# A transformer layer's first microseconds: the first norm's weights as one small row spread by TensorE, blocks in pairs, and transposes of the identity in between

## What is computed

```python
def _rmsnorm(x, g):
    y = x32 * lax.rsqrt(jnp.mean(x32 * x32, axis=-1, keepdims=True) + EPS)
    return (y * g.astype(jnp.float32)).astype(x.dtype)
...
    h = _rmsnorm(x, norm1_g)
    proj = jnp.einsum('bsd,de->bse', h, w_in)
    q, k, v, xr, gate = jnp.split(proj, [...], axis=-1)
```

## Time and profile before

| | |
|---|---|
| median of 3 runs | 1037.27 us |
| the profiled execution, its own time | 1037.77 us |
| its span, first to last instruction | 1035.8 us |
| TensorE busy in the span | 984.3 us (95%) |
| VectorE busy | 816.8 us (79%) |
| ScalarE busy | 745.8 us (72%) |

### The profile page before, as it was taken

One profiled execution on the slowest core, in us unless ns is written; L12 is line 12 of the kernel. 1 busy time (PEld: TensorE's weight loads), 2 busy tenths in 40 slices (PEclk: granted clock), 3 DMA queues, 4 the chain that ended last, 5 costly groups with the idle time before them and its releaser, 6 DMA issues.

```text
span 1035.8 us, 15188 instructions
## 1 busy us (share of the span) xinstructions
PE 984.3 (95%) x5051; PEld 825.9 (80%) x5051; DVE 816.8 (79%) x1084; ACT 745.8 (72%) x1004; POOL 336.8 (33%) x176
## 2 busy tenths in 40 slices
PE   5999999999999999949999999999999999999995
PEld 4997998877877888738888888888888888888874
DVE  5759898989885225777988988898889888988883
ACT  6448888488995555547877887797779777977773
POOL 1100000043792111140425642563366336503321
PEclk9999999999999999969999999999999999999998
DMA  8110111001102733379999999999999999999842
GB/s 285 38 47 6 46 42 42 0 2 62 62 1 84 274 113 118 129 268 412 409 392 391 410 392 392 391 411 392 391 389 401 388 390 387 399 385 364 307 168 35
DMA packets 75409, 248.97 MB, mean 240 GB/s; under 512 B 9396, under 2 KB 16616, under 8 KB 75368
## 3 DMA queue, kind: packets, MB, share of 16 engines
q1 hardware_dynamic: 70616, 231.65, 58.0%
q0 software_dynamic: 4752, 16.78, 6.5%
HBM read 231.63 MB, written 16.78 MB: 240 GB/s over the span
## 4 chain that ended last, share of the span: by engine, by line
PE 83%; DVE 7%; ACT 4%; issue 3%; POOL 1%; DMA 1%; ACTq 0%; SPq 0%; POOLq 0%; DVEq 0%
PE bank L1005 25%; PE bank L1007 24%; PE bank L1006 24%; PE bank L1011 5%; DVE e_lo L1687 2%; ACT e_hi L930 2%; PE bank L1187 1%; PE bank L1153 1%; PE bank L1154 1%; DMA x_nat<-in_x_prompt_dram 1%; PE bank L1040 1%; POOL prob L635 1%; POOL wo_lo L627 0%; DMA xs<-h_rows,idx_all 0%; DVE xc L1456 0%
## 5 line engine op out<-in xcount | busy, mean ns | idle before, releaser
L1005 PE MATMUL bank<-e_hi,xsT_hi 128*128 128x512 f32 x512 | 200.9, 392 | 1.2 <-DVE xsT_lo L1692 1.0
L1007 PE MATMUL bank<-e_hi,xsT_lo 128*128 128x512 f32 x512 | 199.3, 389 | 0.0
L1006 PE MATMUL bank<-e_lo,xsT_hi 128*128 128x512 f32 x512 | 199.3, 389 | 0.0
L667 POOL COPY idx_now<-idx_all 128x1 uint32 (+1 forms) x15 | 156.9, 10460 | 21.9 <-DMA y_dram<-ys,idx_now 21.9
L930 ACT ACTIVATE e_hi<-raw_gate 128x1024 fp32r<-128x1024 f32 x128 | 134.6, 1061 | 33.2 <-PE bank L1007 31.7
L1687 DVE TENSOR_TENSOR e_lo<-raw_down,e_hi 128x1024 fp32r<-128x1024 f32 x128 | 146.9, 1218 | 2.3
L1687 DVE TENSOR_TENSOR e_lo<-raw_up,e_hi 128x1024 fp32r<-128x1024 f32 x128 | 146.7, 1214 | 1.5 <-ACT e_hi L930 1.5
L1687 DVE TENSOR_TENSOR e_lo<-raw_gate,e_hi 128x1024 fp32r<-128x1024 f32 x126 | 145.7, 1216 | 2.5 <-ACT e_hi L930 2.5
L930 ACT ACTIVATE e_hi<-raw_up 128x1024 fp32r<-128x1024 f32 x128 | 126.5, 1058 | 1.7 <-PE bank L1007 0.3
L930 ACT ACTIVATE e_hi<-raw_down 128x1024 fp32r<-128x1024 f32 x128 | 125.1, 1058 | 1.3 <-PE bank L1007 1.2
L1005 PEld LDWEIGHTS bank<-e_hi,xsT_hi 128*128 128x128 f32 x512 | 96.1, 188 | 21.6 <-DVE xsT_lo L1692 1.2
(11 more groups left out here) (247 smaller groups left out, 2235.8 us busy)
## 6 DMA issues: line engine op xcount, KB each, us to landing
raw_gate<-in_exp_w_gate_dram SPq DMA_DIRECT2D x64, 1024.0 KB, 12.4
raw_up<-in_exp_w_up_dram SPq DMA_DIRECT2D x64, 1024.0 KB, 9.0
raw_down<-in_exp_w_down_dram SPq DMA_DIRECT2D x64, 1024.0 KB, 8.3
w_raw<-in_w_in_dram SPq DMA_DIRECT2D x6, 1024.0 KB, 5.4
wo_raw<-in_w_out_dram SPq DMA_DIRECT2D x8, 512.0 KB, 4.1
y_dram<-x SPq DMA_DIRECT2D x8, 512.0 KB, 5.1
h_rows<-h SPq DMA_DIRECT2D x8, 512.0 KB, 2.7
x_nat<-in_x_prompt_dram SPq DMA_DIRECT2D x4, 512.0 KB, 7.8
```

What stands on the lines that cost most here:

```text
L667: pool.tensor_copy(idx_now[:, 2:3], idx_all[:, bass.ds(e, 1)] if not isinstance(e, int) else idx_all[:, e:e + 1]).then_inc(idx_copied, 1)
L1005: pe.matmul(out, l_hi, r_hi, start=first, stop=False)
L1006: pe.matmul(out, l_hi, r_lo, start=False, stop=False)
L1007: return pe.matmul(out, l_lo, r_hi, start=False, stop=last)
```

## The change

The load of `g1b` by SyncE is gone. ScalarE, as its first instruction, issues a load of the same 1024 weights as 8 rows of 128 (`g1_rows`). TensorE transposes them to a [128, 8] tile, VectorE copies that to SBUF (`g1_cols`), and TensorE transposes each column, read as a 128 by 128 tile with the column repeated, so that banks 2 and 3 hold the weights on every partition. The norm of blocks 0 to 3 reads them from PSUM; ScalarE then copies them to `g1b` (step `gain`), and blocks 4 to 7 read that. SyncE loads all eight blocks ahead of the second weights and the vector rows. The list of steps takes the blocks in pairs. GpSimd makes the identity before its other constants. `keep_busy(n)` is new: n transposes of the identity into bank 0, whose result nobody reads; there are 6, 14, 4 and 14 of them.

```diff
@@ -128,6 +128,8 @@
     g1b = at("g1b", SM, [P, D], F32)
+    g1_rows = at("g1_rows", SM + 12 * K, [D // P, P], F32)
+    g1_cols = at("g1_cols", SM + 12 * K + 512, [P, D // P], F32)
@@ -299,22 +301,21 @@
-    steps = [("square_x", 0), ("norm_x", 0), ("square_x", 1), ("norm_x", 1), ("turn_x", 0), ("turn_x", 1),
-             ("w_hi", 0, 0), ("w_lo", 0, 0), ("hi_x", 0), ("lo_x", 0), ("w_hi", 0, 1), ("w_lo", 0, 1)]
-    for b in range(2, NB + 1):
-        if b < NB:
-            steps += [("square_x", b), ("norm_x", b)]
-        steps += [("hi_x", b - 1), ("lo_x", b - 1)]
-        if b < NB:
-            steps.append(("turn_x", b))
-        if b == 3:
-            steps.append(("vectors",))
-        if b == 6:
-            steps += [("w_hi", 1), ("w_lo", 1)]
-        steps.append(("project_pair", b - 2))
-        if b == 6:
-            steps += [("empty", 0), ("empty", 1)]
-    steps += [("project_pair", NB - 1), ("empty", 2), ("conv", 0)]
+    GAIN_FROM = 4
+    AHEAD = (6, 14, 4, 14)
+    steps = [("square_x", 0), ("norm_x", 0), ("turn_x", 0), ("square_x", 1), ("norm_x", 1), ("keep_busy", AHEAD[2]), ("turn_x", 1),
+             ("keep_busy", AHEAD[3]), ("w_hi", 0, 0), ("w_lo", 0, 0), ("hi_x", 0), ("lo_x", 0), ("hi_x", 1), ("lo_x", 1),
+             ("w_hi", 0, 1), ("w_lo", 0, 1), ("project_pair", 0), ("square_x", 2), ("norm_x", 2), ("square_x", 3), ("norm_x", 3)]
+    for b in range(2, NB, 2):
+        steps += [("turn_x", b), ("turn_x", b + 1)]
+        if b + 2 < NB:
+            steps.append(("square_x", b + 2))
+        steps += [("hi_x", b), ("lo_x", b), ("hi_x", b + 1), ("lo_x", b + 1)]
+        if b == 2:
+            steps.append(("gain",))
+        if b + 2 < NB:
+            steps += [("norm_x", b + 2), ("square_x", b + 3),  ("norm_x", b + 3), *([("vectors",)] if b == 4 else []), ("project_pair", b - 1), ("project_pair", b)]
+    steps += [("w_hi", 1), ("w_lo", 1), ("project_pair", 5), ("empty", 0), ("empty", 1), ("project_pair", 6), ("project_pair", 7), ("empty", 2), ("conv", 0)]
@@ -499,19 +500,16 @@
         load_x(0)
-        sp.dma_start(g1b[:, :], norm1_g[0:1, :].to_broadcast([P, D])).then_inc(g1_loaded, 16)
         load_x(1)
...
-        for b in range(2, BPS):
+        for b in range(2, NB):
             load_x(b)
         sp.dma_start(w1_raw[:, :, :], w_in[0, :, GROUPS[1][2]:GROUPS[1][2] + GW].rearrange("(k p) n -> p k n", p=P)).then_inc(w1_loaded, 16)
         for at_row, rows_in in rows:
             sp.dma_start(vec_rows[at_row:at_row + rows_in.shape[0], :], rows_in).then_inc(vec_loaded, 16)
-        for b in range(BPS, NB):
-            load_x(b)
@@ -600,12 +598,12 @@
         pool.memset(eps, EPS).then_inc(pool_ready, 1)
+        pool.wait_ge(ident_zeroed, 1)
+        pool.affine_select(out=ident[:, :], in_=ident[:, :], compare_op=ALU.not_equal, fill=1.0, base=0,
+                           pattern=[[-1, P]], channel_multiplier=1).then_inc(pool_ready, 1)
...
-        pool.wait_ge(ident_zeroed, 1)
-        pool.affine_select(out=ident[:, :], in_=ident[:, :], compare_op=ALU.not_equal, fill=1.0, base=0,
-                           pattern=[[-1, P]], channel_multiplier=1).then_inc(pool_ready, 1)
@@ -732,6 +730,7 @@
+        act.dma_start(g1_rows[:, :], norm1_g[0].rearrange("(c p) -> c p", p=P)).then_inc(g1_loaded, 16)
@@ -742,6 +741,10 @@
+            elif kind == "gain":
+                act.wait_ge(xn_ready, GAIN_FROM)
+                act.wait_ge(vec_t, 2)
+                act.activation(g1b[:, :], bank[:, 2:4, :].rearrange("p a b -> p (a b)"), ACT.Copy).then_inc(vec_copied, 1)
@@ -1027,9 +1030,24 @@
-        pe.wait_ge(pool_ready, 5)
+        def keep_busy(n):
+
+            for _ in range(n):
+                pe.transpose(bank[:, 0, 0:P], ident[:, :], ident[:, :])
+
+        pe.wait_ge(pool_ready, 2)
+        keep_busy(AHEAD[0])
+        pe.wait_ge(g1_loaded, 16)
+        pe.transpose(bank[:, 1, 0:D // P], g1_rows[:, :], ident[0:D // P, 0:D // P]).then_inc(vec_t, 1)
+        pe.wait_ge(vec_copied, 1)
+        for c in range(D // P):
+            ins = pe.transpose(bank[:, 2 + c // 4, c % 4 * P:(c % 4 + 1) * P], g1_cols[:, c:c + 1].to_broadcast([P, P]), ident[:, :])
+        ins.then_inc(vec_t, 1)
+        keep_busy(AHEAD[1])
@@ -1043,6 +1061,8 @@
                 pe.wait_ge(ht_lo_done, BPS * (t + 1))
+                if arg[0] in (4, 5):
+                    pe.wait_ge(vec_copied, arg[0] - 2)
@@ -1053,8 +1073,8 @@
                 pe.wait_ge(vec_loaded, 6 * 16)
+                pe.wait_ge(vec_copied, 2)
                 pe.transpose(bank[:, 3, 0:VECS], vec_rows[:, :], ident[0:VECS, 0:VECS]).then_inc(vec_t, 1)
-                pe.wait_ge(vec_copied, 1)
@@ -1382,7 +1402,9 @@
-        dve.wait_ge(g1_loaded, 16)
+        dve.wait_ge(vec_t, 1)
+        dve.tensor_copy(g1_cols[:, :], bank[:, 1, 0:D // P]).then_inc(vec_copied, 1)
+        dve.wait_ge(vec_t, 2)
@@ -1392,8 +1414,11 @@
+                if b >= GAIN_FROM:
+                    dve.wait_ge(vec_copied, 2)
+                gain = bank[:, 2:4, :].rearrange("p a b -> p (a b)") if b < GAIN_FROM else g1b[:, :]
                 dve.scalar_tensor_tensor(out=x_norm[:, b % 2, :], in0=x_nat[:, b, :], scalar=rstd1[:, b:b + 1],
-                                         in1=g1b[:, :], op0=ALU.mult, op1=ALU.mult).then_inc(xn_ready, 1)
+                                         in1=gain, op0=ALU.mult, op1=ALU.mult).then_inc(xn_ready, 1)
```

More of the change, by code:

```diff
@@ L1028, in turn_heads @@
             transposes(turn_bank(n), pieces, qkT_done)
-        pe.wait_ge(pool_ready, 5)
+        def keep_busy(n):
[10 more added lines that the diff above has]
+        keep_busy(AHEAD[1])
         for step in steps:
             kind, arg = step[0], step[1:]
+            if kind == "keep_busy":
+                keep_busy(*arg)
             if kind == "turn_x":
@@ L1415, in _ @@
             elif kind == "vectors":
-                dve.wait_ge(vec_t, 1)
+                dve.wait_ge(pool_ready, 5)
+                dve.wait_ge(vec_t, 3)
                 dve.tensor_copy(vecs[:, :], bank[:, 3, 0:VECS]).then_inc(vec_copied, 1)
-                dve.wait_ge(vec_copied, 1)
+                dve.wait_ge(vec_copied, 3)
             elif kind == "softplus":
```

## The result

The changed kernel takes 1031.82 us, the median of 4 runs (1031.07 to 1032.55), beside 1037.38 for the kernel before (4 runs, 1036.99 to 1038.49). The ratio is 0.9945, with an interval of 0.9934 to 0.9957: 5.6 us faster, 0.55%. The prediction said 1032.0.

A forecast was written before the change was run, and what follows sets the result against it. VectorE was taken to hold back TensorE's first product. Stage's end: 12.8 + 28.34 + 0.1 + 0.2 + 0.5 = 41.9 against 47.23, 5.3 us less, so 1032.0 us; range 1031.0 to 1036.2.

The forecast's parts named there:

- The weights' row: Start: row lands at 4.0, weights in PSUM at 6.3, VectorE starts at 6.4 instead of 6.60; by itself 0.2 us.
- the early end that the range had named: Start: a row landing at 2.5 leaves block 0's root as the bound, 0.9 us better, 1031.1.
- No broadcast in the queue: SyncE's loads: without 1.4 us of broadcast, block 1 lands near 5.5, the weights' halves near 6.9 and 8.3.
- The order: VectorE's chain from 6.4: two norms, `w_lo`, two `lo_x` to 12.7; first product at 12.8 instead of 17.61.
- The transposes of the identity: TensorE before pair 0: clock rises at about 9.4, fillers end at 12.8, cost nothing, and pair 0 runs at high level.
- TensorE from there: First product to stage's end: six turned blocks and eight pairs, 28.34 us, plus 0.1 for vectors and 0.7 of waits.
- What lies beside: Weights' copy sits in ScalarE's slack, at most 1.0 us; vector rows arrive in time; 5.3 us carries to the end.
- The clock stays low until real products have run: Rival, chance 0.20: identity transposes burden the start, pair 0 at 16.1, 1.3 us gained, 1036.0.
- a late rise: Rival, chance 0.14: at the start the clock rises between 11 and 16 us; 2.1 to 4.5 gained, near 1034.
- The row lands late: Rival, chance 0.05: the weights' row lands at 9.7 behind SyncE's traffic, pair 0 at 21.6, 4.4 us lost, 1041.7.
- Theory A: Start: earlier first product from order, row and loads together is the gain; identity transposes keep the clock from costing 1 to 2 us.

The follow-up runs named there:

- broadcast: The changed kernel with the norm's weights loaded as before, by a broadcast read between blocks 0 and 1, without row, spread and copy: 1033.05 us.
- again2: The changed kernel itself, unedited, measured once more beside the version without transposes of the identity: 1031.39 us.
- old_order: The changed kernel with the list of steps of the kernel before; row load, early block loads and identity transposes stay: 1035.35 us.
- loads_back: The changed kernel with blocks 4 to 7 loaded last again, behind the second weights and the vector rows: 1033.40 us.
- none: The changed kernel without any transpose of the identity (all four counts 0): 1033.61 us.
- no_last: The changed kernel without the last 14 transposes of the identity, those behind block 1: 1032.39 us.
- order_only: The kernel before with only the new list of steps and the identity made first; broadcast and old load order stay: 1035.44 us.
- none2: The changed kernel without any transpose of the identity, measured a second time: 1033.05 us.

## Why the prediction was right

The forecast's mechanism and size held: 41.9 for the stage's end, measured 42.03, and 5.2 us carried to the program's end. Inside, four terms were off. VectorE started 0.8 us sooner than put, its chain took 1.2 longer and TensorE's work behind it 0.3 less; that this cancels to 0.1 is luck, as the two other profiles of the changed kernel (41.58 and 41.12) show.

*The weights' row* was there by 3.00 (2.54 and 2.72 where nothing stands ahead of its transpose), not 4.0. VectorE started at 5.60, not 6.4, held by block 0's root: this is the early end that the range had named. In again2 the sum for VectorE can be read with no load in the way: 6.46 us from its start to pair 0, put at 6.4. The broadcast kernel shows the part's worth, 1.4 to 2.3 us, where "by itself" 0.2 was written for the start alone; the rest is block 1's landing, costed under *No broadcast in the queue*.

*No broadcast in the queue* was the weak step. Block 1 was there by 5.40, as put, but the first half of the weights was put at 6.9 and landed at 8.39, in the other executions with this order of loads at 7.0 to 8.3. I took one rate, 378 GB/s from 8 to 10 us. From 4 to 6 us the loads of the kernel before move 227; the landings shown there, block 0 at 4.04 and the half megabyte of the broadcast at 6.60, tell the same. In the changed kernel the rate of that stretch differs between executions, 269 in the first and 382 in again2, where the weights landed at 7.0, as put:

```profile
4.00:6.00 2.00, 2.00 (x15) 2.00 (x14) 0.37 (x2) 1.96 (x4) 0.00 (x0) 1.00 0.87 269
```

```profile
4.00:6.00 2.00, 2.00 (x14) 2.00 (x13) 0.17 (x1) 1.75 (x4) 0.00 (x0) 1.00 1.03 382
```

*The order:* VectorE's chain, 0.8 us early at its start, lost 1.02 to that landing: 13.16 in place of 12.8. The steps themselves ran as costed, and norms that read PSUM take 1.28 us, no more than before.

*The transposes of the identity:* the assumption was a rise near 9.4. It came near 5.2, and in six other runs with the same first transposes between that and 8.2. With the changed kernel's list none of these moments holds up pair 0, because VectorE is the bound until then, as the step said. What hides the transposes is real: doubled, they cost 1.4 to 2.3 us.

*TensorE from there* took 28.87 us and not 29.14. Of the small waits allowed, 0.7, the trace lists none. What came in their place, 0.4 above 28.44, lies for the most part in the turning: blocks 2 and 3 took 1.78 us (16.14 to 17.92) and blocks 4 and 5 1.84 (23.76 to 25.60), put at 1.58 each.

*What lies beside:* the vector rows land near 21.3 by the wait in old_order, 4.3 us before the changed kernel asks for them; block 4 would have been late (loads_back). Behind the stage the program is the same, and TensorE's one wait up to 195 us is again the 0.8 us for ScalarE.

The rivals. *The clock stays low until real products have run* and *a late rise* are both refuted for the profiled executions: before 13.16 TensorE had done transposes only, and fourteen of them took 1.69 us. The Trainium skill, TensorE: Matmul & The Clock Gate, Part 4, has it that the full clock doesn't engage for transposes; in this kernel it does, and the measurement decides. Its other half, that a transpose doesn't count as busy in the same way, isn't refuted: the level rose earlier with products as filler (by 4.92) than with transposes (5.2 to 8.2). *The row lands late* fell away. The rule of the Trainium skill, DMA: Bandwidth & Descriptors, Queues, rings and completion order, by which an engine takes its queues in turn, packet by packet, agrees with the trace: the row, on a queue of its own, landed at 2.54 in the run none, ahead of block 0, which ScalarE got at 4.21.

Theory A held, but for one part: what the identity's transposes save shows in the times and not in the profiles' starts. What stays open: why the kernel without the identity's transposes takes 1.5 us more in the median while its two profiled executions reach the stage's end as early. What I hold likely, and didn't show: its clock rose only just ahead of pair 0 (near 10.9 or later in none), the moment of the rise varies by 3 us between executions (5.2 to 8.2 with the fillers), and an execution in which it comes later runs pair 0 at the low level. At 0.09 us for each of 14 or 15 products, as in no_last and order_only, that is an estimated 1.3 us. The granted clock on record can't settle it, since its column reads 1.00 before the first rise, whatever the level. Open too is the price of the last fourteen in the whole time.

## What to carry to other kernels

When a load leaves the head of a queue, work out at the rate of that very stretch when each load behind it lands, for the next of them can become the bound; and take a range for the rate (269 to 382 GB/s here), since it differs between executions. An order of steps and an order of loads are one decision: here the earlier blocks cost 2.2 us under the old list and save about 0.7 under the new one, in one profile each. Filler on TensorE is free only while it ends before the engine that it waits for, counted at the low clock. In the profile of no_last it pays by keeping the pause before the first product short; in the times only all four fillers together show a gain.

## What the hardware showed that I had not expected

- TensorE's granted level rises on transposes alone, at a moment that differs between executions of the same start: near 5.2 us in one, near 8.2 in another. With products in place of the filler's transposes it had risen by 4.92, in the one execution seen.
- It fell after a pause of 3.17 us, with two products still at the high level, and didn't after pauses of 1.71 (none2), 2.02 (the changed kernel) and 2.59 us (old_order, ahead of block 2's transposes). That is one execution each.
- A product of two f32 tiles of 128 by 128 takes two instructions, 2.93 us for six where six transposes take 1.54.
- The column of the granted clock reads 1.00 from 0 to 47 us in the kernel before, although products there run 0.213 us apart: ahead of the first rise the spacing of equal instructions tells the level, and the column doesn't. A fall behind that rise it does show, 0.50 in no_last.
- The loads' rate from 4 to 6 us is 227 to 382 GB/s over the runs here; from 8 to 10 us it is 374 to 423.
